# Weights of the last gated layer cast once into DRAM during the MLP before it, and loaded plain by each tile

## The reference, cut to what matters

```python
def mixer_a(h, w_in, b_in, vn_g, vn_b, w_s, b_s, w_out):
    z = gelu(h @ w_in + b_in)              # (S, 2*3072)
    u, v = split(z, 2)                     # 3072 each
    v = layernorm(v, vn_g, vn_b)           # chunks of 128 positions, 8 groups of 384
    gate = einsum('gts,bcsgd->bctgd', tril(w_s), v) + b_s
    return (u * gate) @ w_out

for i in range(4):
    x = x + mixer[i % 3](rmsnorm(x, norm_mix[i]), ...)
    x = x + square(relu(rmsnorm(x, norm_mlp[i]) @ w1[i])) @ w2[i]
return rmsnorm(x, norm_final)
```

## Time and profile before

| what | value |
|---|---|
| median of three runs | 3090.28 us (3086.88 to 3092.50) |
| the profiled execution | 3090.11 us |
| its span (core 2, the slowest) | 3088.6 us |
| spans of cores 0 to 7 | 3078.8, 3066.3, 3088.6, 3066.7, 3069.5, 3081.7, 3070.6, 3083.8 us |
| granted clock of core 2 | 0.992 of full speed |
| busy PE / DVE / ACT / POOL | 97% / 76% / 43% / 24% of the span |
| software queue q0 | 328.51 MB, 60.3% of the 16 DMA engines' span |
| hardware queue q1 | 150.10 MB, 13.9% |
| the MLP of layer 2 | to about 2136 us |
| the last gated layer | about 2120 to 2662 us |

### The profile page before, as it was taken

One profiled execution on the slowest core, in us unless ns is written; L12 is line 12 of the kernel. 1 busy time (PEld: TensorE's weight loads), 2 busy tenths in 40 slices (PEclk: granted clock), 3 DMA queues, 4 the chain that ended last, 5 costly groups with the idle time before them and its releaser, 6 DMA issues.

```text
span 3088.6 us, 48893 instructions; the slowest of 8 cores (3066.3 to 3088.6 us)
## 1 busy us (share of the span) xinstructions
PE 2995.5 (97%) x15592; PEld 1500.1 (49%) x15866; DVE 2350.0 (76%) x3939; ACT 1320.5 (43%) x2297; POOL 728.0 (24%) x879
## 2 busy tenths in 40 slices
PE   8999999999999999999998899999999989999998
PEld 4444444444444444444675444444556465644444
DVE  7945767678779987877678788877867778677886
ACT  4312433434644354456533634553322343333554
POOL 1111233101414320132651421212111150101221
PEclk9999999999999999999999999999999999999999
DMA  9699997776767377786765477768697977886684
GB/s 166 109 153 165 166 158 125 166 156 155 170 145 135 56 159 163 159 195 150 161 139 139 101 170 172 166 148 164 145 205 190 180 175 156 214 166 141 151 188 115
DMA packets 157739, 481.76 MB, mean 156 GB/s; under 512 B 13744, under 2 KB 27696, under 8 KB 157488
## 3 DMA queue, kind: packets, MB, share of 16 engines
q0 software_dynamic: 95376, 328.51, 60.3%
q1 hardware_dynamic: 62112, 150.10, 13.9%
HBM read 652.36 MB, written 89.65 MB: 240 GB/s over the span
## 4 chain that ended last, share of the span: by engine, by line
PE 88%; DMA 4%; DVE 3%; issue 2%; ACT 2%; POOL 1%; SPq 0%; DVEq 0%; another core or an unknown queue 0%; ACTq 0%; POOLq 0%
PE bank L164 88%; DMA ring<-a_wp 2%; DMA ring<-a_w_in 1%; DVE xT L164 1%; DMA xT<-x 1%; POOL sacc L164 1%; DVE m_tv L164 0%; DMA ring<-b_w_out 0%; DVE bank L164 0%; ACT sq L164 0%; DVE hT1v L164 0%; ACT mh0v L164 0%; DVE ring L164 0%; DVE mh3v L164 0%; POOL acc L164 0%
## 5 line engine op out<-in xcount | busy, mean ns | idle before, releaser
L164 DVE TENSOR_TENSOR xT<-bank,xT 128x512 f32<-128x512 f32 (+3 forms) x1052 | 735.0, 716 | 270.9 <-PE bank L164 247.2
L164 PE MATMUL bank<-m_tv,ring 128*128 128x512 bf16 (+2 forms) x3666 | 811.2, 373 | 16.2 <-DVE xT L164 10.1
L164 PEld LDWEIGHTS bank<-m_tv,ring 128*128 128x128 bf16 x3724 | 359.3, 98 | 435.7 <-issue 25.6
L164 ACT ACTIVATE bank<-bank 128x512 f32<-128x512 f32 x496 | 289.4, 587 | 426.0 <-PE bank L164 346.4
L164 POOL DMA_DIRECT2D ring<-m_w x256 | 137.5, 537 | 1244.0 <-PE bank L164 1151.7
L164 ACT ACTIVATE m_tv<-bank 128x512 bf16<-128x512 f32 x511 | 302.0, 598 | 45.9 <-DVE bank L164 10.9
L164 DVE TENSOR_TENSOR m_tv<-m_tv,m_tv 128x512 bf16<-128x512 bf16 x494 | 221.1, 478 | 93.6 <-ACT m_tv L164 90.6
L164 POOL TENSOR_TENSOR sacc<-sacc,sq 128x512 f32<-128x512 f32 (+1 forms) x162 | 212.9, 1314 | 250.6 <-ACT sq L164 224.5
L164 DVE TENSOR_TENSOR ring<-ring 128x512 bf16<-128x512 bf16 (+1 forms) x420 | 225.4, 554 | 19.9 <-DMA ring<-m_w 12.1
L164 ACT ACTIVATE sq<-xT 128x512 f32<-128x512 f32 (+1 forms) x252 | 152.8, 621 | 142.1 <-POOL sacc L164 78.9
L164 PE MATMUL bank<-m_hv,ring 128*128 128x512 bf16 x688 | 172.6, 379 | 3.4 <-issue 0.6
(11 more groups left out here) (247 smaller groups left out, 4339.8 us busy)
## 6 DMA issues: line engine op xcount, KB each, us to landing
ring<-a_w_in POOLq DMA_DIRECT2D x85, 1024.0 KB, 16.5
ring<-m_w POOLq DMA_DIRECT2D x132, 512.0 KB, 6.9
m_pre<-ring SPq DMA_DIRECT2D x124, 512.0 KB, 6.1
ring<-m_pre POOLq DMA_DIRECT2D x124, 512.0 KB, 6.8
ring<-m_w POOLq DMA_DIRECT2D x124, 384.0 KB, 5.9
ring<-a_wp SPq DMA_DIRECT2D x112, 384.0 KB, 5.9
ring<-a_w_out POOLq DMA_DIRECT2D x32, 768.0 KB, 8.6
a_wp<-ring SPq DMA_DIRECT2D x12, 896.0 KB, 8.2
```

The source lines that it names most:

```text
L164: return lambda e: getattr(e, _method)(*[_r(a) for a in args], **{k: _r(v) for k, v in kwargs.items()})
```

## The change

The twelve blocks of `a_w_in` of the last gated layer get a bf16 copy in DRAM, `a_wc`. It is written by 24 transfers from DRAM to DRAM (half a block each: 128 rows of 2048 elements, 1 MB read, 512 KB written), issued by POOL. The list `casts` is filled in the MLP of layer 2, the v blocks (6 to 11) first, and from the second pair of `pipe` on (CAST_FROM = 1) each step issues one by `next_cast`. A cast waits for the last PE operation written before it. In the last gated layer `load_cast` takes the place of `load_w`: a plain transfer from `a_wc` to the ring slot, also issued by POOL, that waits for the two casts of its block. The first gated layer is as before.

```diff
+    a_wc = nc.dram_tensor("a_wc", [12, 128, 4096], BF16, kind="Internal").ap()
+    wc_r = [[Res(), Res()] for _ in range(12)]
+    casts = []
+
+    def next_cast():
+
+        if casts:
+            j, c = casts.pop(0)
+            after = next(o.i for o in reversed(sc.ops) if o.eng == "pe")
+            sc.op("pool", I("dma_start", out=a_wc[j, :, c:c + 2048], in_=dram["a_w_in"][1, j, :, c:c + 2048], max_dma_last_dim=8192),
+                  wr=[wc_r[j][c // 2048]], cost=0.75, dma=sc.dma_key(f"wc{j}_{c}"), nbytes=512 * 2048, after=[after], tag="cast", lat=LOAD_LAT)
+
+    def load_cast(j, parts=1):
+        t, r, key = take_slot()
+        rs = r.split(parts) if parts > 1 else [r]
+        n = 4096 // parts
+        for i in range(parts):
+            last_load[0] = sc.op("pool", I("dma_start", out=t[:, i * n:(i + 1) * n], in_=a_wc[j, :, i * n:(i + 1) * n], max_dma_last_dim=8192),
+                                 rd=wc_r[j], wr=[rs[i]], cost=0.75, dma=key if i == 0 else sc.dma_key(f"wcl{ring_n[0]}_{i}"),
+                                 nbytes=256 * n, tag="load")
+            w_ops.append(last_load[0])
+        return t[:].rearrange("p (a b) -> p a b", a=8), rs if parts > 1 else r
...
+    CAST_FROM = 1
...
+        if l == 2 and nxt and not last:
+            casts.extend((k, c) for k in (6, 7, 8, 9, 10, 11, 0, 1, 2, 3, 4, 5) for c in (0, 2048))
         for j, (p, b) in enumerate(pipe):
...
+                if CAST_FROM <= j:
+                    next_cast()
                 step()
...
             def load_v(vp, parts=1, after=()):
+                if self.seven:
+                    return load_cast(6 + vp, parts) + (parts,)
                 return load_w("a_w_in", ia, 6 + vp, (8, 512), after=after, parts=parts) + (parts,)
...
-                            wu, wur = load_w("a_w_in", ia, cj // 4, (8, 512))
+                            wu, wur = load_cast(cj // 4) if self.seven else load_w("a_w_in", ia, cj // 4, (8, 512))
```

## The result

The changed kernel takes 3123.94 us in the median of 6 runs, against 3091.15 us before, 6 runs. The ratio of the undisturbed runs is 1.0104, 95% interval 1.009 to 1.0119, so 33 us more. I had forecast 3083 us. One run of each kernel (3470 us before, 3572 us after) fell into a slower state of the chip; the ratio leaves these two out.

A forecast was written before the change was run, and what follows sets the result against it. PE was taken to bound the kernel, holding 88% of the last-ending chain. From 3090.1 us, minus 13 us gained in the last gated layer, plus 6 us lost in the MLP, gave 3083 us; 8-in-10 range 3072 to 3108 us.

The forecast's parts named there:

- That PE's stalls are all that counts, and the free time of DMA is what is spent: Whole kernel: PE holds 88% of the last-ending chain, so a change pays only where PE stands still or clocks lower.
- The free 18.7 + 14.9 + 43.8 = 77.4 us: MLP of layer 2: unused DMA time in three stretches, 1814 to 1918, to 1966 and to 2112 us.
- A cast costs 3.4 us: MLP of layer 2: DMA time of one DRAM-to-DRAM cast, taken from the m_w load; bounds 1.3 and 6.9 us.
- The lead hides part of it, 6 us: MLP's first stretch, short by 8.5 us: the five ring slots' lead hides part once; 6 us lost, bounds 0 and 8.5.
- The gain of 13 us: Last gated layer, core 2: waits and clock given back, 1.0 + 4.6 + 4.0 + 3.6 us; bounds 5.6 and 17.3.
- what I said for themselves: Last gated layer: DMA share in the v stretch about 0.4 to 0.5 instead of 1.03, no waits for a_w_in.
- where I had said about 4: Last gated layer, slowest core: PE's waits for a_wp would be about 4 us after the change.
- the clock's 3.6 us: Last gated layer: two 20 us slices at granted clock 0.91 would return to 1.00, giving back 3.6 us.
- rival A: Last gated layer: the stalls stay, gain 5.6 us against cost 6, so 3090 us, no change; chance 0.20.
- Rival B: MLP of layer 2: memory is the bound at 324 GB/s, 34 us more, 3111 us in all; chance 0.23.
- waits over 13 us that run on to 2112 us: MLP of layer 2: PE's waits for m_w loads that would show memory to be the bound.
- Planner, POOL's issues, the wait on PE: MLP of layer 2: 13 us of issues on POOL and the casts' wait for PE, priced at nothing; planner not mentioned.

The follow-up runs named there:

- casts alone: Changed kernel with the 24 casts kept but the last gated layer loading and casting float32 as before, the copy unread: 3132.45 us, ratio 1.0136.
- without the planner's knowledge: Changed kernel with the casts' bytes left out of the planner's model (nbytes=0), transfers the same: 3116.91 us, ratio 1.0071 against the kernel before.
- thin loads: Kernel before, no casts or copy, each of the 48 a_w_in loads of the last gated layer moving only 256 columns of a part: 3081.89 us, ratio 0.9979.

## Why the prediction was wrong, step by step

- **That PE's stalls are all that counts, and the free time of DMA is what is spent:** right, and it is the frame in which the rest is seen. The free 18.7 + 14.9 + 43.8 = 77.4 us of the earlier trace rows were right too: casts of half the size (24 x 3.1 = 74 us by their own share) and half as many (12 x 5.1 = 61 us) went in without a loss that can be seen.
- **A cast costs 3.4 us:** this step failed. I took the row of m_w because "the longer side of these transfers is the read". Measured, the landing in DRAM adds 1.3 us: 4.7 us, and 5.1 us by the share of DMA in this MLP. At 4.7 us 24 casts want 113 us, and 35 us are missing in place of 4.2 over the whole stretch. The casts alone cost 42 us. My bounds (1.3 to 6.9 us) held the price, but the range did not follow it: at 4.7 us my own sum gives (37.6 - 18.7) + (18.8 - 14.9) + (56.4 - 43.8) = 35.4 us, and 3090.1 - 13 + 35 = 3112 us, above the range's 3108. The other 12 us up to the measured 3124 are the clock and a gain that was too large, below.
- **The lead hides part of it, 6 us:** this failed with the price. A lead hides a shortfall once. Here it did, while the landing of the stored sums went from 6.6 to 21 us; after that what was missing was PE's. And the longer stalls of PE brought the clock down beside them: 27 us more of waits and up to 10.6 us by the clock on core 7. I had counted the clock on the side of the gain alone.
- **The gain of 13 us:** too large. The plain loads did what I said for themselves (share 0.42 in the v part, no wait for a_w_in), but over all cores the layer gives back 3.5 us, and with next to nothing loaded 6.5 us (3 to 10). I had priced the gain by the stalls of the one slowest core. On that core the waits for a_wp did fall as forecast, from 12.7 to 5.0 us where I had said about 4. But on core 4 they rose from 5.3 to 9.3, on core 7, now the last, they stayed (9.8 and 9.2), and the clock's 3.6 us did not come back there either, as two slices of the layer show it at 0.91 again:

```profile
2520.00:2540.00 20.00, 17.21 (x140) 14.25 (x138) 14.15 (x24) 10.24 (x16) 16.35 (x13) 0.91 0.44 135
2560.00:2580.00 20.00, 17.23 (x91) 9.27 (x91) 10.26 (x16) 6.90 (x12) 9.71 (x10) 0.91 0.71 260
```

  With thin loads 6.1 us for a_wp remain on the slowest core, and 3.9 in the mean over the cores, where 7.4 were before. So about half of these waits is not made by the loads of a_w_in. That these pieces wait for slots and for each other, as rival A has it, fits but was not tested by itself.
- **Rival B** was right in its sign and place: waits over 13 us that run on to 2112 us. It was near in size too. It had 34 us more in the MLP, where the v part starts 37 us later, and 3111 us in all, 21 us more than before against 33 measured; most of that difference is the gain of 13 us, which it had taken over. Its mechanism, bytes read and written in memory together at one rate, is borne out only in part: reading and writing DRAM in one transfer is dearer than either, but 2.9 of the 4.8 us of a cast are there with no DRAM in it. So its nearness is partly luck. The Trainium skill, HBM Reference, Specifications (TRN2), gives about 358 GB/s for each core when both cores of a pair stream. The float32 copy from DRAM to DRAM moved 10 x 2.1 = 21.0 MB in 59.9 us on core 5, 350 GB/s (338 to 366 over the eight cores), which agrees within 6%. The cast to DRAM moved 15.7 MB in 49.5 us, 318 GB/s. By 358 GB/s this MLP would have become 2 us longer, as the prediction estimated from that page. A price for each kind of transfer would have told the loss, one rate for all did not.
- **Planner, POOL's issues, the wait on PE:** priced at nothing, and nothing large is there (half casts at the same places, 0.9993; the loss in the MLP without the planner's knowledge); a few us of the planner's order stay open.

## What to carry to other kernels

Free time of a shared resource is a budget: add up what the new transfers want, each at a measured price for its own source and destination, and past the budget count each us as lost, with the clock's share on top. If that price is not known, let the range follow its bounds. A copy that is made once and read four times saves bytes in the sum and can still lose, if it is made where the feed has no room and used where the feed was not what PE waited for; the same idea at half the dose (v blocks alone, every second step) won 0.3% in three of four timings. Before pricing a gain, ask whose bytes a late transfer stood behind, and look at all cores, not at the slowest alone; the version with the loads thinned out bounds the gain in one run.

## What the runs showed of the hardware

- All eight cores at once, per transfer of 128 x 2048 elements, on core 5 (the slowest): cast chip to chip 2.9 us, DRAM to chip 3.6 to 3.7, DRAM to DRAM 4.8 to 4.9; plain bf16 2.1 to the chip, 3.1 from DRAM to DRAM, 2.2 to DRAM; float32 DRAM to DRAM 6.0 (ten in a row, start to start, their turnaround included). A cast from the chip to DRAM landed as fast as one from chip to chip.
- A DMA share of 0.96 over 280 us cost PE nothing (half casts), and with one of 1.00 PE was idle for 21 of 280 us (casts alone): the ring hid queueing nearly up to the full feed, and no further.
- The granted clock of core 7 was 0.91 or 0.83 in five slices of the MLP, each of which holds one wait of PE of 2.8 to 4.9 us. Behind the wait of 4.90 us, for instance, eight matmuls took 3.25 us, where eight took 1.89 behind the short waits. This put up to 10.6 us on top of 27 us of added waits.
